# Attention of a four-layer backbone: the max pass interleaved one unit ahead and evenly, the output accumulated in 65 columns by three short matmuls, two output banks in turn

## The reference

```python
s = (jnp.einsum('bqhd,bkhd->bhqk', qn, k_nope, preferred_element_type=F32)
     + jnp.einsum('bqhr,bkr->bhqk', qr, k_rope, preferred_element_type=F32)) * scale
p = jax.nn.softmax(s, axis=-1)
return jnp.einsum('bhqk,bkhd->bqhd', p.astype(v.dtype), v)
...
return (o.reshape(B, T, BRANCH) * jax.nn.silu(gate)) @ w_out
```

## Time and profile before

| what | value |
|---|---|
| median of 3 runs | 3885.57 us (3880.24 to 3885.69) |
| profiled execution, its own time | 3885.78 us |
| span of its trace | 3884.0 us |
| PE busy | 3544.3 us, 91% of the span |
| PEld busy | 2040.4 us, 53% |
| DVE busy | 2490.0 us, 64% |
| ACT busy | 2190.3 us, 56% |
| POOL busy | 1091.3 us, 28% |
| granted TensorE clock, mean | 0.984 |

### The profile page before, as it was taken

One profiled execution on the slowest core, in us unless ns is written; L12 is line 12 of the kernel. 1 busy time (PEld: TensorE's weight loads), 2 busy tenths in 40 slices (PEclk: granted clock), 3 DMA queues, 4 the chain that ended last, 5 costly groups with the idle time before them and its releaser, 6 DMA issues. The chain is left out here.

```text
span 3884.0 us, 71972 instructions
## 1 busy us (share of the span) xinstructions
PE 3544.3 (91%) x27916; PEld 2040.4 (53%) x27916; DVE 2490.0 (64%) x3536; ACT 2190.3 (56%) x2859; POOL 1091.3 (28%) x931
## 2 busy tenths in 40 slices
PE   6999899999999988999899988888999998898888
PEld 3554455555455555555555555555555445555544
DVE  6436677777357468888655428886642667777744
ACT  5424677777444358888733227776333457676761
POOL 0000344444220025555521002223200014444442
PEclk9999999999999999999999999999999999999999
DMA  6227433232112342332012434332112652222111
GB/s 250 64 86 228 105 76 82 57 83 63 63 34 76 113 125 62 74 71 67 23 68 72 124 101 101 97 96 58 52 51 90 187 145 42 57 47 57 41 52 60
DMA packets 375890, 330.05 MB, mean 85 GB/s; under 512 B 247168, under 2 KB 294976, under 8 KB 374112
## 3 DMA queue, kind: packets, MB, share of 16 engines
q1 hardware_dynamic: 375648, 326.66, 31.1%
HBM read 235.37 MB, written 91.23 MB: 84 GB/s over the span
## 5 line engine op out<-in xcount | busy, mean ns | idle before, releaser
L798 PE MATMUL bank<-H_hilo,w_hilo 128*128 128x512 f16 (+1 forms) x5760 | 1044.7, 344 | 11.0 <-DVE w_hilo L1048 7.8
L2309 ACT ACTIVATE p_f<-bank 128x1024 f32<-128x1024 f32 (+2 forms) x768 | 744.1, 969 | 485.2 <-PE bank L2247 421.1
L2247 PE MATMUL bank<-q_slots,k_slots 96*128 96x512 f16 (+7 forms) x3968 | 949.2, 369 | 7.4 <-PEq L1199 4.4
L2062 DVE TENSOR_REDUCE max_parts<-bank 128x1 f32<-128x512 f32 (+1 forms) x1248 | 795.7, 663 | 247.7 <-PE bank L1993 240.3
L798 PEld LDWEIGHTS bank<-H_hilo,w_hilo 128*128 128x128 f16 x5760 | 563.4, 98 | 492.1 <-DVE w_hilo L1048 8.8
L2313 ACT ACTIVATE p_hi<-bank 128x1024 f16<-128x1024 f32 (+2 forms) x768 | 741.1, 965 | 0.0
L2427 POOL TENSOR_TENSOR p_lo<-p_f,p_hi 128x1024 f16<-128x1024 f32 x240 | 534.5, 2227 | 648.4 <-ACT p_hi L2313 648.4
L2374 DVE TENSOR_TENSOR p_lo<-p_f,p_hi 128x1024 f16<-128x1024 f32 (+1 forms) x528 | 599.8, 1137 | 156.7 <-ACT p_hi L2313 155.8
L1993 PE MATMUL bank<-k_slots,q_slots 96*128 96x512 f16 (+4 forms) x1392 | 487.5, 372 | 70.8 <-DVE max_parts L2062 53.4
L2247 PEld LDWEIGHTS bank<-q_slots,k_slots 96*128 96x128 f16 (+2 forms) x3968 | 369.1, 99 | 314.5 <-issue 29.1
L2216 PE MATMUL bank<-cq_hilo,p_hi 128*128 128x129 f16 x3200 | 338.8, 221 | 37.9 <-ACT o_lo_hi_den L2327 22.7
(11 more groups left out here) (207 smaller groups left out, 3721.6 us busy)
## 6 DMA issues: line engine op xcount, KB each, us to landing
ada_w<-in_w_ada SPq DMA_DIRECT2D x48, 768.0 KB, 6.2
gate<-z_ring SPq DMA_DIRECT2D x32, 640.0 KB, 3.3
gate_rows<-gate SPq DMA_DIRECT2D x32, 640.0 KB, 4.0
q_slots<-q_mla SPq DMA_DIRECT2D x64, 240.0 KB, 3.2
k_mla<-H_hilo SPq DMA_DIRECT2D x64, 224.0 KB, 3.2
k_slots<-k_mla SPq DMA_DIRECT2D x64, 224.0 KB, 4.4
cq_hilo<-v_scratch SPq DMA_DIRECT2D x64, 224.0 KB, 4.1
v_lo_hi_one<-v_scratch SPq DMA_DIRECT2D x64, 224.0 KB, 4.3
```

What stands on the lines that cost most here:

```text
L798: ins = pe.matmul(dst, lhs(a, k), rhs(b, k), start=(k == 0 and n == 0), stop=(k == nk - 1 and n == 2))
L2062: dve.tensor_reduce(mx[:, par, t, c:c + 1], entry_bank(b, k)[:, 0:n], AX.X, ALU.max).then_inc(s_red.h, 1)
L2247: ins = pe.matmul(dst, lhs, rhs, start=(m == 0), stop=(m == len(ops) - 1), skip_group_check=swa)
L2309: act.activation(p32[:, p % 2, 0:cols], src, ACT.Exp, scale=scale).then_inc(s_p32.h, 1)
```

## The change

- **Max pass.** The entries of a head are no longer one list a head ahead. `own[j]` are entries of the current head in step j, `ahead[j]` of the next head. In MLA and GQA unit 0's entries and the first five of unit 1 stand in steps 4 to 12 of the head before, the rest of unit 1 and the context unit in steps 0 to 3 of the head itself; every step has two or three entries. The first is issued between the two key blocks of a step's scores, the second behind the scores, others behind `pv`; DVE takes the first two ahead of `p_lo`.
- **SWA** now uses both max banks in turn: a context part (512 columns) and a local part (256 or 384) for each query tile, each with its own reduction.
- **Output.** `pv` makes three matmuls for a tile, 65, 64 and 65 columns, which add up in the same 65 columns of one bank. `OB` becomes two banks used by alternate units, and `pv` waits for the copy two units back. ACT's copy has 260 columns and stands between the two exponentials. POOL's addition is gone.
- **p_lo on POOL** also for step 1 in MLA and GQA, and for steps 0, 2, 4 and 6 in SWA.
- **Loads.** The rotary keys of MLA are loaded for the first two heads only.

```diff
-        OB = bank[3]
+        OB = [bank[3][:, 0], bank[3][:, 1]]
...
-            base = c_ + a_[:lag] + [("turn", 2)] + a_[lag:] + b_[:lag] + [("turn", 0)] + b_[lag:]
...
+            own = [b_[4:6], b_[6:8] + c_[:1], c_[1:] + [turn(1)], [turn(2)], [], [], [], [], []]
+            ahead = [[], [], a_[:1], a_[1:2], a_[2:4], a_[4:7], a_[7:] + b_[:1], [turn(0)] + b_[1:3], mod + b_[3:4]]
         else:
...
+            own = [b_[5:7], b_[7:9] + c_[:1], c_[1:] + b_[9:11], b_[11:] + [turn(2)], [turn(1)]] + [[]] * 8
+            ahead = [[]] * 4 + [a_[:2], a_[2:4], a_[4:6], a_[6:8], a_[8:10], a_[10:] + b_[:1], mod + b_[1:2],
+                                [turn(0)] + b_[2:3], b_[3:5]]
...
-        pooled = [] if swa else [3, 5, 7, 9, 11]
+        pooled = [0, 2, 4, 6] if swa else [1, 3, 5, 7, 9, 11]
...
-                    if first and above_zero(i * 6 + un):
-
-                        pe.wait_ge(s_ev.h, s_ev.base + i * 6 + un)
...
-                                pe.matmul(o, ph[:, slot[q], sel], V[:, b, kt, 0:VC], start=fresh[half], stop=False,
-                                          skip_group_check=True)
-                                fresh[half] = False
-                                ins = pe.matmul(o[:, HD:VC], pl[:, slot[q], sel], V[:, b, kt, HD:VC], start=False,
-                                                stop=True, skip_group_check=True)
+                    if first and above_zero(i * 6 + un - 1):
+
+                        pe.wait_ge(s_ev.h, s_ev.base + i * 6 + un - 1)
...
+                            o = OB[un % 2][:, t * (HD + 1):(t + 1) * (HD + 1)]
+                            sel = slice(off + j * P, off + j * P + P)
+                            pe.matmul(o, ph[:, slot[q], sel], V[:, b, kt, HD:VC], start=fresh, stop=False,
+                                      skip_group_check=True)
+                            fresh = False
+                            pe.matmul(o[:, 0:HD], ph[:, slot[q], sel], V[:, b, kt, 0:HD], start=False, stop=False,
+                                      skip_group_check=True)
+                            ins = pe.matmul(o, pl[:, slot[q], sel], V[:, b, kt, HD:VC], start=False, stop=True,
+                                            skip_group_check=True)
...
+                                if n == 0:
+                                    for k in todo[:1]:
+                                        emit_entry(pe, i, b, k)
+                            scored.then_inc(s_sc.h, 1)
+                            for k in todo[1:2]:
+                                emit_entry(pe, i, b, k)
...
-                    pool.tensor_tensor(hi, hi, lo, ALU.add).then_inc(s_sum.h, 1)
-                    pool.wait_ge(s_sum.h, s_sum.base + n + 1)
```

More of the change, by code:

```diff
@@ L1790, in attention @@
+        order = [e for step in ahead for e in step] + [e for step in own for e in step]
+        NE = len(order)
+        NM = NE - 3 - ada
+        stream, at_step = [[], []], [[], []]
         for b in range(2):
             for j in range(NS):
[L1792 to L1795 removed]
@@ new lines, in attention @@
+                if j in out_step[b]:
+                    made.append((0, ("out", out_step[b][j])))
+                at_step[b].append(list(range(len(stream[b]), len(stream[b]) + len(made))))
+                stream[b] += made
+        count = lambda k, which: sum(e[0] in which for e in order[:k])
+        nmax = [count(k, ("max",)) for k in range(NE + 1)]
+        nturn = [count(k, ("turn",)) for k in range(NE + 1)]
+        turns = [e[1] for e in order if e[0] == "turn"]
+        turn_order = {u: n for n, u in enumerate(turns)}
@@ new lines, in attention, with head_of, items @@
+        ring = [(b, n) for b in range(2) for n in range(len(stream[b]))]
+        ring += [None] * (-len(ring) % R)
+        place = {bn: n for n, bn in enumerate(ring) if bn}
+        before_all = [e for step in ahead for e in step]
+        def head_of(i, b, n):
+            b += stream[b][n][0]
+            return i + b // 2, b % 2
+        def items(b, j, last):
+            if last and b == 1:
+                return [n for n in at_step[b][j] if stream[b][n][0] == 0 and stream[b][n][1][0] != "out"]
+            return at_step[b][j]
@@ L1815, in attention, with entry_bank @@
+        def entry_bank(i, b, n):
+            if isinstance(i, int) and i < 0:
+                return MB[sum(d for d, e in stream[b][:n]) % 2]
+            return MB[place[b, n] % R]
         P2 = 2 * NS
@@ new lines, in wait_bank @@
+        def wait_bank(pe, i, b, n):
+            if isinstance(i, int) and i < 0:
+                earlier = [m for m in range(n) if stream[b][m][0] == 1]
+                if len(earlier) >= 2:
+                    wait_taken(pe, i, b, earlier[-2])
+                return
+            m = place[b, n]
+            while True:
+                m -= R
+                if m < 0:
+                    m, i = m + len(ring), i - 1
+                if isinstance(i, int) and i < 0:
+                    pe.wait_ge(s_red.h, s_red.base + sum(e[0] == "max" for e in before_all))
+                    pe.wait_ge(s_mr.h, s_mr.base + sum(e[0] == "turn" for e in before_all))
+                    return
+                if ring[m] is not None and wait_taken(pe, i, *ring[m]):
+                    return
```

390 lines of the change are left out of this document (161 added, 229 removed).

## The result

| kernel | median, us | runs | ratio to before, 95% interval |
|---|---|---|---|
| before | 3882.9 | 3878.83 to 3885.69 | 1 |
| changed | 4028.64 | 4024.44 to 4040.6 | 1.038 [1.0355, 1.0407] |

What follows compares the result with a forecast made beforehand. PE, busy 91% of the span, was taken as the bound, with 257.3 us of waits mostly in attention. Heads -184, tiles +9, value-phase entries -8 gave -183: 3885.8 to 3703 us, range 3635 to 3810.

Steps and rivals of the forecast that it cites:

- Turns, outs and max banks: PE's waits at a head's border and max pass: most of 27.7, 21.2 + 35.8 and 53.4 + 13.5 us go.
- Three short matmuls: In pv, one more matmul and weight load for each of 5728 tiles, priced at 1.5 ns each: +9 us.
- The first rival: Three matmuls with weight loads in pv not issued at column rate, 0.043 each: +246 us, 3940 us; chance 0.10.
- The price of a tile: Time of a pv tile on PE: 0.086 us now, 0.086 to 0.09 after, with starts 27 to 30 ns apart.
- Two output banks: pv waits for the copy of two units back, so PE's output-copy waits of 22.7 + 25.3 us go.
- The collision on DVE: Step 2: neg_max of the context unit waits up to 1.9 us behind POOL's p_lo; PE loses about 1.1 us an MLA head.
- An entry's bank: Max pass: entries two a step, half the scores or a pv apart, remove most of PE's 53.4 + 13.5 us bank waits.
- The floors of a head: PE's time a head without waits: first MLA layer 32.5 us, GQA 27.3, SWA 19, last MLA layer 31.5.
- Loads and the value phases: Rotary-key waits of 11.7 us go; ten first-head entries leave each value phase, -2 us a layer, -8 in all.
- The second, waits coming back through POOL: All three neg_max a head caught by POOL and p_lo late: 96 us more, 3799 us; chance 0.22.
- The third (the collision does not happen): PE comes near its floor, no collision in step 2: 70 us less, 3633 us; chance 0.13.
- the fourth (nothing is won): ACT's and POOL's chain sets the pace in all layers: 3885 us; chance 0.02.

Runs made afterwards that it cites:

- written out: All pairs of heads of the MLA layers coded one by one without the loop; kernel before with new output this way: 3873.34 us, without new output 3877.93 us.
- the best kernel: Changed kernel with row copy between exponentials, turn of unit 1 in step 3, POOL's p_lo steps as before, MLA pair loops unrolled: 3786.7 us, 0.9749.
- the rows early: Changed kernel with ACT copying turned rows of negated maxima between a step's two exponentials, not behind both: 3904.57 us, 1.0054.
- With 853 a round: Kernel before with only the new output (three matmuls a tile, two output banks, 260-column copy between exponentials, no POOL addition), loop kept: 3939.98 us, 1.0155.

## Why the prediction was wrong

- **The step that failed first is "Turns, outs and max banks".** It counted each max bank as free once DVE had reduced it, and said that nothing needs the turn of unit 1 for six steps. True of the row, but not of the bank: a turn is itself an entry and holds a bank until ACT's copy. Before, the copy was late as well, but where the turns stood no entry wanted that bank so soon: no wait on `q_slots` stands in the earlier trace rows. With max entries spread over all steps, two or three a step, the next entry of that bank comes behind the `pv` of the turn's step or in the middle of the next scores. The order on ACT would have shown it: the copy behind `p_f` and `p_hi`, 2 x 1.02 us. The forecast had 2.0 to 4.5 us a head gained in all, most of it here; the runs showed 155 us of new waits, worth 124 in time by moving the copy and 22 more by moving the turn.
- **The second failure is one of omission.** "Three short matmuls" was priced by what PE executes, +9 us. It had no term for what PE has to be fed: the body of an MLA pair, near 855 matmuls with a weight load each, no longer goes round without being fetched again, and stalls at each jump back. Cost: 82 us, in the MLA phases alone. The first rival named the same edit as the danger, but by another mechanism, and would have had PE slow in every tile.
- **The price of a tile was right, and its size a little low.** Warm, `pv` starts at 551.47 and 551.56 lie 0.09 apart, and eight tiles took 0.73 us from 3564.98 to the next scores at 3565.71, 0.091 a tile where 0.086 stood before. The forecast was 1.5 ns more, the rows give 5: 29 us for 9. The first rival (0.12 and more) is refuted.
- **Two output banks: right that the waits on the copy go** (48.0 us before). What it left out is that this and the tiles about cancel: written out, the new output gains 5 us in all.
- **The collision on DVE was right in place and length** and priced too high. Between 3561.19 and 3563.32 POOL runs p_lo of step 1, `neg_max` of the context unit takes 1.43 us from 3561.92, and step 3's first entry is late by 0.52 us of PE (1.1 was the forecast). In time, p_lo of step 1 back on DVE gave only 3 and 2 us in the two MLA layers, some 0.2 a head. These are the rows:

```profile
3561.19 2.13 POOL L2414 TENSOR_TENSOR p_lo<-p_f,p_hi 128x1024 f16<-128x1024 f32 x1 [6.34 <-ACT p_hi L2316]
3561.92 1.43 DVE L2069 TENSOR_SCALAR neg_max<-max_rows 128x2 f16<-128x2 f32 x1
3563.99 0.39 PE L2003 MATMUL bank<-k_slots,q_slots 96*128 96x512 f16 x1 [0.52 <-DVE max_parts L2058]
```

  The Trainium skill (SBUF — State Buffer, section Who interferes with whom) has this as a rule, the later of the two being blocked for the whole instruction. The rows agree: `neg_max` of the context unit takes 1416 ns on average with p_lo of step 1 on POOL, 172 with it on DVE.
- **"An entry's bank"** should have given back most of 53.4 + 13.5 us. Waits on `max_parts` were 96.1 after, and 59.6 in the best kernel. Moving p_lo back to DVE took 19 us of them (80.1 to 61.0 with the rows early), but the turns' waits on the same reductions rose by 15; what makes the rest was not tried by itself.
- **The floors of a head held as floors, the rest above them was priced too low in GQA and SWA.** In the best kernel, which is not the forecast one, a head takes 35.3, 33.1, 23.2 and 34.5 us in the four layers, where 34.5, 30.3, 21.8 and 33.7 were forecast. MLA is within 0.8 us. SWA is off by 1.35 a head, GQA by 2.8, 45 us a layer: ACT does wait for POOL's p_lo there, as the forecast had it, but the length of that chain, 30 us, was too short. Which part of this is POOL, which DVE with 433 of 530 us busy, stays open; p_lo in another split between the two was tried only in step 1 and SWA.
- **Loads and the value phases.** PE's 11.7 us of waits for the rotary keys went to 0.2, as forecast. Ten entries fewer in each value phase were to give 8 us; outside the attention phases 2 were gained.
- **The clock** had a place in the prediction only as something regained. It went the other way, as each new stall took some of it: the mean was 0.984 before, 0.97 after.

The rivals: the first forecast the sign and missed the mechanism (chance 0.10). The second, waits coming back through POOL, is real in kind, with at most 20 us of its 96. The third (the collision does not happen) is refuted by the rows; it also took 1.1 us off all 64 heads, though the sum had charged it in the 32 of MLA alone; the fourth (nothing is won) missed that time could be lost. The chance of slower, 0.11, rested on one price of one instruction; that a bank could be held by a third engine, or that code could be too long for its loop, was in no case.

## What to carry to other kernels

When entries of a shared bank are moved closer together, list every kind of entry and for each the last reader of the bank, and look at where that reader stands in its own engine's order: a short copy behind two long instructions holds the bank for all three. When instructions are added to the body of a hardware loop, look for waits of PE on "issue" once per round of the loop, and compare with the body written out or with a shorter body, and look whether q8 is silent while the loop runs; the price of the instructions alone does not tell. And an edit of several parts is worth taking apart even when it is slower: here 4029 us held a 3787 us kernel, four small edits away.

## What was not expected of the hardware

- A loop on PE with some 855 matmuls and weight loads a round stalls 4.1 to 4.6 us at each of its ten jumps back and is fetched again in every round; one with 654 (the kernel before) waits 0.2 us at most and is fetched no more while it runs, and the same long body does not stall when written out. With 853 a round eight of ten jumps stall, and over the two that do not, q8 is silent. Removing the loop gained nearly twice the stalls, 82 us for 44; over the 3.8 us behind the first stall the granted clock is 0.50.
- Written out, the changed kernel moves 4.36 MB of instructions, less than the 4.83 MB with the loop.
- Three matmuls of 64 and 65 columns with a weight load each start 30 ns apart on average, close to the rate of their columns.
